# Loading expert weights in halves of 1 MB: one decoder layer on one Trainium2 core

## Chip, cores and metric

The kernel runs on one core of one Trainium2 chip. The metric is device time in microseconds (us) of one execution, the median over several. "The profiled execution" is one further execution, recorded by the hardware profiler; its span runs from the first to the last recorded instruction.

## What is computed

One layer of a decoder trunk: 256 tokens of 1024 float32 numbers, a conditioning vector `c`, a mixer (causal pooling beside a gated DeltaNet), then a mixture of experts, then a last RMSNorm. The change lies in the mixture of experts:

```python
def moe_ffn(h, router_w, router_b, w1, b1, w2, b2):
    logits = xt @ router_w + router_b                 # (256, 32)
    top_val, top_idx = lax.top_k(logits, 4)
    comb = softmax(top_val)
    ...                                               # tokens grouped by expert into blocks
    def expert_block(args):
        hu = xb @ w1[e] + b1[e]                       # w1[e]: 1024 x 2048
        x_glu = minimum(hu[:, 0::2], 7.0)
        x_lin = clip(hu[:, 1::2], -7.0, 7.0)
        act = x_glu * sigmoid(1.702 * x_glu) * (x_lin + 1.0)
        return act @ w2[e] + b2[e]                    # w2[e]: 1024 x 1024
    ...                                               # sum over experts, weighted by comb
```

All 32 experts have tokens, so all their weights are read: 12 MB (12.6 million bytes) for each expert, 403 MB in all, float32.

## The kernel before

**Staging.** Five engines run their own programs and meet at semaphores. All large weights pass through one SBUF buffer, `ring`: `RING` = 6 slots of 2 MB (128 partitions of 16 KB). SyncE issues the loads into it, in the order in which TensorE uses them. The front of the kernel (modulation, projections, mixer) takes 30 chunks through the ring, five uses of each slot (`USES` = 5). Then `stream(e, blocks_before)` loads one expert: slots 0 to 3 hold w1, two of its eight k-columns each (input features p*8+c, so one partition's two columns are 16 KB in a row in DRAM), slots 4 and 5 hold w2, half of its rows each, in two parts of 8 KB a partition.

**Semaphores.** `landed[s]` rises by 16 with each load into slot s, `used[s]` by 1 each time TensorE is done with it. SyncE waits for `used[s]` at the number of blocks before this expert plus `USES`, and issues the load (L503, L504). TensorE waits for `landed[s]` at 16 times the uses so far (L1343, L1365). The last expert's slots 3 and 5 are an exception: they are loaded in two halves of 1 MB (L501, L502), the second with a semaphore of its own, `hidden_in` and `last_in`.

**Order of the work.** The router's result is turned into a list of blocks of up to 64 tokens, in SBUF, on the chip (`blocks_i`); an expert with more than 64 tokens has a second block, which finds its weights in the ring. In this input there are 33 blocks for 32 experts (66 gates of two a block in the trace). TensorE runs `serve(n)` for each: the bias product, four `w1_chunk`s of eight products each (L1338; two records each in the trace, so "x16" is a chunk and "x64" a block's w1), `gather` of the next block's tokens (L1309), `combine` of the block before (L1384), the turns of selection, activation and next tokens (L1402, L1322, L1316), and two `w2_chunk`s of eight products (L1372). VectorE and ScalarE compute the gates between: the first gate when bank 0 is complete (`pe_hu`), the second when `used[3]` says that bank 1 is. `serve_last` is the last block, in a slightly other order. Expert 0's block stands before the loop, mixed with the last steps of routing.

**Small loads.** SyncE also loads the expert biases (`b_in`, four loads) and the last norm's weights (`fin_g`, semaphore `fin_in`); at the very start `c` (`c_in`) and the identity (`const_in`).

Of the kernel before, what the change touches and what calls it, by code (L numbers as in the profile page):

```python
# [24 lines left out]
P = 128  # L25
# [14 lines left out]
E = 32  # L40
# [3 lines left out]
RING = 6  # L44
# [13 lines left out]
ROW_C = 0  # L58
# [54 lines left out]
def program(nc, x, c, ada_w, ada_b, norm_mix_g, norm_ffn_g, w_in, conv_w, pool_w, pool_scale, a_log,  # L113
            dt_bias, gdn_norm_g, w_pool_out, w_gdn_out, w_out, router_w, router_b, exp_w1, exp_b1,
            exp_w2, exp_b2, final_norm_g, const, out):
    with ExitStack() as ctx:
# [148 lines left out]

        const_in = sem("const_in")
        rows_in = sem("rows_in")
        c_in = sem("c_in")
        tables_in = sem("tables_in")
        x_in = sem("x_in")  # L270
        early_in = sem("early_in")
        b_in = sem("b_in")
        fin_in = sem("fin_in")
        hidden_in = sem("hidden_in")
        last_in = sem("last_in")
        out_done = sem("out_done")
        landed = [sem(f"landed{i}") for i in range(RING)]
        upper_in = [sem(f"upper_in{i}") for i in range(2)]
        used = [sem(f"used{i}") for i in range(RING)]

        vec_chain = sem("vec_chain")
# [191 lines left out]

        @block.sync
        def _(sp):
            sp.dma_start(rows[ROW_C:ROW_C + 8, :], c.rearrange("b (r n) -> (b r) n", n=P)).then_inc(c_in, 16)
            sp.dma_start(consts[:, 0:2 * P + 1], const[:, 0:2 * P + 1]).then_inc(const_in, 16)
            for t in range(T):
                sp.dma_start(xt[:, t, :], x[0, t * P:(t + 1) * P, :]).then_inc(x_in, 16)
            for n, (kind, src) in enumerate(chunks):  # L480
                if n >= RING:
                    sp.wait_ge(used[n % RING], n // RING)
                dst = ring[:, n % RING, :, :]
                if kind in parts_of:
                    dst = slot_as(n % RING, parts_of[kind])
                if n in chunk_no["qkv"][:2]:
                    sp.dma_start(dst[:, 0:4, :], src[:, 0:4, :]).then_inc(upper_in[n - 2], 16)  # L487
                else:
                    sp.dma_start(dst, src).then_inc(landed[n % RING], 16)
                if n == RING - 1:  # L490
                    for m in chunk_no["qkv"][:2]:
                        sp.dma_start(ring[:, m, 4:8, :], chunks[m][1][:, 4:8, :]).then_inc(landed[m], 16)
                if n == RING - 1:
                    sp.dma_start(consts[:, 2 * P + 1:CONST_W], const[:, 2 * P + 1:CONST_W]).then_inc(tables_in, 16)

            def stream(e, blocks_before):
                for s in range(RING):
                    src = w1_dram[e, :, 2 * s:2 * s + 2, :] if s < 4 else w2_dram[e, s - 4]
                    sp.wait_ge(used[s], blocks_before + USES)
                    if isinstance(e, int) and e == E - 1 and s in (3, 5):  # L500
                        sp.dma_start(slot_as(s, 2)[:, 0, :], src[:, 0, :]).then_inc(landed[s], 16)  # L501
                        sp.dma_start(slot_as(s, 2)[:, 1, :], src[:, 1, :]).then_inc(hidden_in if s == 3 else last_in, 16)  # L502
                    else:  # L503
                        sp.dma_start(slot_as(s, 2), src).then_inc(landed[s], 16)  # L504

            stream(0, 0)
            sp.wait_ge(vec_x1, 4)
            for i in range(2):
                at = slice(i * SLOTS, i * SLOTS + E)
                sp.dma_start(b1_rows[at, :], exp_b1[0][:, i * D:(i + 1) * D]).then_inc(b_in, 16)  # L510
                sp.dma_start(b2_rows[at, :], exp_b2[0][:, i * 512:(i + 1) * 512]).then_inc(b_in, 16)
            sp.dma_start(fin_g, final_norm_g.partition_broadcast(P)).then_inc(fin_in, 16)
            sp.wait_ge(vec_route, 1)
            with sp.Fori(1, E - 1) as e:
                stream(e, first_block_of(sp, e))
            stream(E - 1, first_block_of(sp, E - 1))
            for i in range(2 * T):
                cut_ = slice((i % 2) * 512, (i % 2 + 1) * 512)
                sp.wait_ge(vec_out, i + 1)
                sp.dma_start(out[0, (i // 2) * P:(i // 2 + 1) * P, cut_], fin[:, i // 2, cut_]).then_inc(out_done, 16)  # L520
            sp.wait_ge(out_done, 16 * 2 * T)
# [267 lines left out]
        def _(pe):  # L789
# [41 lines left out]
                if i % 2:  # L831
                    mm.then_inc(pe_adacol, 1)

            pe.wait_ge(const_in, 16)
            pe.wait_ge(c_in, 16)
            nc.tensor.transpose(bank[7][:, 0:8], rows[ROW_C:ROW_C + 8, :], ident[0:8, 0:8]).then_inc(pe_c, 1)
            def keep_warm(times, b):

# [500 lines left out]
                                          slot_as(q, 2)[:, i, lo:lo + 512], start=False, stop=(c == KC - 1))  # L1339
                return mm  # L1340

            def w1_chunk(n, q, e=0, last=False):
                pe.wait_ge(landed[q], 16 * (e + USES + 1))  # L1343
                if q < 3:
                    for i in range(2):
                        for b in range(2):
                            mm = hidden(n, q, i, b)
                    mm.then_inc(used[q], 1)
                elif last:
                    for b in range(2):  # L1350
                        hidden(n, q, 0, b)
                    pe.wait_ge(hidden_in, 16)
                    hidden(n, q, 1, 0).then_inc(pe_hu, 1)
                    hidden(n, q, 1, 1).then_inc(used[q], 1)
                else:
                    for i in range(2):
                        mm = hidden(n, q, i, 0)
                    mm.then_inc(pe_hu, 1)
                    for i in range(2):
                        mm = hidden(n, q, i, 1)  # L1360
                    mm.then_inc(used[q], 1)

            def w2_chunk(n, b, e, last=False):
                pe.wait_ge(act_actT, 2 * n + b + 1)
                pe.wait_ge(landed[4 + b], 16 * (e + USES + 1))  # L1365
                for h in range(2):
                    if last and b and h:
                        pe.wait_ge(last_in, 16)
                    for c in range(2):
                        for o in range(2):  # L1370
                            lo = c * D + o * 512
                            mm = nc.tensor.matmul(bank[2][o * SLOTS:(o + 1) * SLOTS, :], actT[:, b, c, h, :],  # L1372
                                                  slot_as(4 + b, 2)[:, h, lo:lo + 512],
                                                  start=(b + h + c == 0), stop=(b + h + c == 3))
                mm.then_inc(used[4 + b], 1)

            def combine(n, last=False):

# [45 lines left out]
            def serve_last(n):  # L1424
                e = E - 1
                bias(n)
                w1_chunk(n, 0, e)
                w1_chunk(n, 1, e)
                combine(n - 1)
                w1_chunk(n, 2, e)  # L1430
                turn_sel(n)
                w1_chunk(n, 3, e, last=True)
                keep_warm(5, 3)
                turn_act(n, 0)
                keep_warm(2, 3)
                pe.wait_ge(act_selT, n + 1)
                w2_chunk(n, 0, e)
                turn_act(n, 1)
                w2_chunk(n, 1, e, last=True)

            keep_warm(2, 0)
            pe.wait_ge(pool_h2, 1)
# [3 lines left out]
                             start=True, stop=True).then_inc(pe_route, 1)  # L1446
            turn_x(0)
            keep_warm(2, 0)
            pe.wait_ge(b_in, 16 * 4)
            bias(0)  # L1450
            w1_chunk(0, 0)
            pe.wait_ge(vec_blocks, 2)
# [19 lines left out]
        def _(dve):  # L1472
# [375 lines left out]
            copy(blocks_i[:, 2 * P:2 * P + E], bank[6][0:1, 32:32 + E])  # L1848
            copy(blocks_i[:, 0:2 * P], bank[6][0:1, 64:64 + 2 * P]).then_inc(vec_route, 1)
            dve.wait_ge(act_gt2, 1)  # L1850
            dve.wait_ge(b_in, 16 * 4)
            for h in range(2):
                at = slice(h * SLOTS, h * SLOTS + E)
                ins = tt(b2_rows[at, :], b2_rows[at, :], gt2_row[at, :], ALU.mult)
# [18 lines left out]
            def serve(n, last=False):  # L1873
                e, start = (0, 0) if isinstance(n, int) else (expert_of(dve, n), start_of(dve, n))
                if not last:
                    e_next, start_next = expert_of(dve, n + 1), start_of(dve, n + 1)
                at_least(dve, pe_selT, n)
                for t in range(T):
                    ins = ts(wsel[:, t], slots[:, bass.ds(start, SLOTS)].unsqueeze(1).to_broadcast([P, 2, SLOTS]),  # L1879
                             slot_of[:, t, bass.ds(e, 1)], gatew[:, t, bass.ds(e, 1)], ALU.is_equal, ALU.mult)  # L1880
                ins.then_inc(vec_wsel, 1)
                dve.wait_ge(pe_gather, n + 1)
                if not last:
                    select(e_next, start_next)
                dve.wait_ge(pe_hu, n + 1)
                gated(n, 0)
                dve.wait_ge(used[3], n + USES + 1)
                gated(n, 1)
                if not last:
                    dve.wait_ge(pe_gather, n + 2)  # L1890
                    mark(e_next)
                dve.wait_ge(used[5], n + USES + 1)
                tt(y_nat, bank[2][:, :], gt2_row, ALU.mult).then_inc(vec_y, 1)  # L1893

            dve.wait_ge(vec_route, 1)
# [24 lines left out]
            add_experts(1, 0)  # L1920
            add_experts(1, 1)
            half_of_squares(1)
            dve.wait_ge(fin_in, 16)
            scale_out(0)
            scale_out(1)

# [26 lines left out]
```

## Time and profile before

| what | us |
|---|---|
| median of 3 runs | 1356.93 (1356.05 to 1356.97) |
| the profiled execution | 1355.68 |
| its span | 1353.3 |
| TensorE busy | 1282.3 (95% of the span) |
| VectorE, ScalarE, GpSimd busy | 391.3, 188.2, 48.3 |
| chain that ended last | TensorE 54%, DMA 42% |
| mean rate of all loads | 349 GB/s, 471.71 MB |

The page's rows by slice cut the span into 40 equal parts of 33.8 us. Busy shares add up over stages with different limits; the chain that ended last follows, from the last instruction back, what released each. A line such as L1338 is that of kernel.py. The granted TensorE clock is 0.997 of full speed over the span. "Landing" is the moment at which the last of the 16 DMA engines has raised the semaphore of a load.

### The profile page before, as it was taken

The page shows a single profiled execution, that of the slowest core. Times are in us where ns is not written, and L with a number is a line of the kernel's source. Part 1 is how long each engine was busy: PE and PEld are TensorE (multiplying, and loading weights), DVE is VectorE, ACT ScalarE, POOL GpSimd, SP SyncE. Part 2 cuts the span into 40 slices and gives each one's busy share as a digit, 9 for nine tenths or more (in the row PEclk, how much of TensorE's full clock was granted, in tenths as well). Part 3 has the DMA queues.
Part 4 walks back from the last instruction along what each step waited for, and adds up shares of the span by engine and source line. Part 5 has one row for each costly group of instructions (what it writes and reads, how often), then busy time and mean ns, then how long its engine had stood idle before and what let it go on. Part 6 is the DMA issues. An engine that isn't in the chain of part 4 may idle for free.

```text
span 1353.3 us, 17457 instructions
## 1 busy us (share of the span) xinstructions
PE 1282.3 (95%) x6549; PEld 624.1 (46%) x6550; DVE 391.3 (29%) x982; ACT 188.2 (14%) x401; POOL 48.3 (4%) x48
## 2 busy tenths in 40 slices
PE   7999999999999999989999998999999999999997
PEld 5788878898653333223333322333333322333332
DVE  1599574732252211112111111211211111121112
ACT  1110223422120110001100000100010000011001
POOL 1020012220000000000000000000000000000000
PEclk9999999999999999999999999999999999999999
DMA  9998550008349999999999999699999999999996
GB/s 334 357 375 299 206 187 1 1 27 316 124 152 407 426 426 426 425 426 426 428 426 426 426 425 426 253 427 423 426 429 426 426 427 425 426 425 429 427 426 248
DMA packets 69079, 471.71 MB, mean 349 GB/s; under 512 B 4093, under 2 KB 4410, under 8 KB 36154
## 3 DMA queue, kind: packets, MB, share of 16 engines
q1 hardware_dynamic: 68224, 469.62, 84.5%
q10 hardware_dynamic: 538, 1.13, 0.3%
q0 software_dynamic: 288, 0.55, 0.2%
q8 instruction: 21, 0.34, 0.1%
q14 instruction: 8, 0.07, 0.0%
HBM read 470.23 MB, written 1.05 MB: 348 GB/s over the span
## 4 chain that ended last, share of the span: by engine, by line
PE 54%; DMA 42%; DVE 1%; SPq 1%; ACT 1%; issue 1%; DVEq 0%
DMA ring<-in_exp_w_dram 40%; PE bank L1338 18%; PE bank L806 12%; PE bank L1372 6%; PE bank L1235 2%; DMA ring<-in_ada_w_dram 2%; PE bank L1024 2%; PE bank L1384 2%; PE bank L1309 2%; PE bank L900 1%; PE bank L1330 1%; PE bank L1157 1%; PE bank L1141 1%; PE bank L1154 1%; SPq L487 1%
## 5 line engine op out<-in xcount | busy, mean ns | idle before, releaser
L1338 PE MATMUL bank<-ring,work 128*64 128x512 f32 x2112 | 470.6, 596 | 47.3 <-DMA ring<-in_exp_w_dram 47.3
L1338 PEld LDWEIGHTS bank<-ring,work 128*64 128x64 f32 x2112 | 144.6, 137 | 368.9 <-issue 272.2
L1372 PE MATMUL bank<-ring,work 128*64 128x512 f32 x1056 | 234.1, 595 | 0.9 <-ACT work L749 0.5
L1372 PEld LDWEIGHTS bank<-ring,work 128*64 128x64 f32 x1056 | 72.9, 137 | 137.9 <-issue 136.6
L756 ACT ACTIVATE work<-work 128x256 f32<-128x256 f32 x66 | 27.5, 416 | 765.1 <-DVE work L1863 765.1
L1863 DVE TENSOR_SCALAR work<-bank 128x256 f32<-128x256 f32 x66 | 27.6, 419 | 350.4 <-PE bank L1338 350.4
L806 PE MATMUL bank<-region_h,ring 128*128 128x256 f32 x576 | 126.6, 380 | 0.0
L806 PEld LDWEIGHTS bank<-region_h,ring 128*128 128x128 f32 x576 | 108.8, 190 | 14.4
L1893 DVE TENSOR_TENSOR work<-bank,work 128x512 f32<-128x512 f32 x33 | 22.8, 692 | 313.8 <-PE bank L1372 313.8
L1384 PE MATMUL bank<-work 64*128 64x512 f32 x264 | 65.6, 615 | 0.8 <-DVE work L1893 0.8
L1309 PE MATMUL bank<-qkv,work 128*64 128x512 f32 x264 | 62.3, 592 | 0.2 <-DVE work L1801 0.2
L1879 DVE TENSOR_SCALAR work<-consts,region_z 128x128 f32 (+1 forms) x66 | 19.9, 345 | 87.7 <-issue 87.7
L1870 DVE TENSOR_TENSOR work<-work 128x256 f32<-128x256 f32 x66 | 40.7, 617 | 12.3 <-DVE work L1866 12.3
L1384 PEld LDWEIGHTS bank<-work 64*128 64x128 f32 x264 | 22.7, 186 | 43.2 <-issue 41.5
L1309 PEld LDWEIGHTS bank<-qkv,work 128*64 128x64 f32 x264 | 19.0, 137 | 37.4 <-issue 37.4
L1330 PE MATMUL bank<-work 32*64 32x512 f32 x264 | 35.9, 612 | 0.3 <-issue 0.3
L1505 DVE SCALAR_TENSOR_TENSOR region_z<-ring,c_act,region_z 128x512 f32<-128x512 f32 x48 | 35.6, 809 | 0.0
L1538 DVE SCALAR_TENSOR_TENSOR qkv<-bank,conv_cols,qkv 128x255 f32<-128x255 f32 (+2 forms) x72 | 31.3, 477 | 1.3
L900 PE MATMUL bank<-region_h,ring 128*128 128x256 f32 x128 | 28.8, 382 | 1.3 <-DVE region_h L1523 1.3
L1024 PE MATMUL bank<-region_h,ring 128*128 128x256 f32 x128 | 29.6, 379 | 0.0
L806 PE MATMUL bank<-region_z,ring 128*128 128x256 f32 x128 | 27.9, 380 | 1.0 <-DVE region_z L1736 1.0
L1866 DVE SCALAR_TENSOR_TENSOR work<-work 128x256 f32<-128x256 f32 x66 | 28.0, 425 | 2.3
(304 smaller groups left out, 953.6 us busy)
## 6 DMA issues: line engine op xcount, KB each, us to landing
ring<-in_exp_w_dram SPq DMA_DIRECT2D x190, 2048.0 KB, 23.6
ring<-in_ada_w_dram SPq DMA_DIRECT2D x12, 2048.0 KB, 12.4
ring<-in_w_in_dram SPq DMA_DIRECT2D x11, 2048.0 KB, 12.8
ring<-in_w_in_dram SPq DMA_DIRECT2D x4, 1024.0 KB, 17.2
ring<-in_w_gdn_out_dram SPq DMA_DIRECT2D x2, 2048.0 KB, 11.7
ring<-in_w_out_dram SPq DMA_DIRECT2D x2, 2048.0 KB, 16.6
ring<-in_exp_w_dram SPq DMA_DIRECT2D x4, 1024.0 KB, 23.5
ring<-in_w_pool_out_dram SPq DMA_DIRECT2D x1, 2048.0 KB, 8.4
```

The source lines that it names most:

```text
L806: mm = nc.tensor.matmul(out_ap, w(k) if w else w_slot(n, j, k), rhs[:, k, :], start=(k == 0), stop=(k == kc - 1))
L900: mm = nc.tensor.matmul(pair(i)[:, a, :], w_slot(n, 2 * (i % 2) + a, k), hT[:, k, :], start=(k + a == 0), stop=(k == KC - 1), skip_group_c ...
L1024: mm = nc.tensor.matmul(pair(7)[:, a, :], w_slot(n, j, k), hT[:, k, :], start=(k == 0), stop=(k == KC - 1))
L1309: mm = nc.tensor.matmul(bank[3][h * SLOTS:(h + 1) * SLOTS, :], sel[:, t, :], h2[:, t, h * 512:(h + 1) * 512], start=(t == 0), stop=(t == T ...
L1330: nc.tensor.matmul(bank[b][h * SLOTS:(h + 1) * SLOTS, :], onehot[b * SLOTS:b * SLOTS + E, :], b1_rows[b * SLOTS:b * SLOTS + E, h * 512:(h ...
L1338: mm = nc.tensor.matmul(bank[b][h * SLOTS:(h + 1) * SLOTS, :], xT[:, c % 4, c // 4, :], slot_as(q, 2)[:, i, lo:lo + 512], start=False, sto ...
L1372: mm = nc.tensor.matmul(bank[2][o * SLOTS:(o + 1) * SLOTS, :], actT[:, b, c, h, :], slot_as(4 + b, 2)[:, h, lo:lo + 512], start=(b + h + c ...
L1384: mm = nc.tensor.matmul(bank[4 + 2 * t + h][:, :], wselT[at, t * P:(t + 1) * P], y_nat[at, :], start=False, stop=last, skip_group_check=True)
L1505: ins = stt(half, w[:, k, :], c_act[:, k:k + 1], half, ALU.mult, ALU.add)
L1538: steps.append(stt(qkv[:, f, shift:S], src[:, a, 0:S - shift], w, qkv[:, f, shift:S], ALU.mult, ALU.add))
L1866: stt(lin[:, b, :], lin[:, b, :], 1.0, glu[:, b, :], ALU.add, ALU.mult).then_inc(vec_lin, 1)
L1870: tt(act_nat[:, b, :].rearrange("q (c p) -> q p c", c=2), lin[:, b, :].rearrange("q (p c) -> q p c", c=2), sig[:, b, :].rearrange("q (p c) ...
```

## The change

Each of the 32 experts' six slots is now loaded in two halves of 1 MB, and freed in two halves. A half of a w1 slot is one k-column, 128 rows of 8 KB that are 64 KB apart in DRAM; a half of a w2 slot is one of its two parts. The first half's load raises `landed[s]`, the second's a new semaphore `late_in[s]`, one for each slot. TensorE waits for each half by itself and raises `used[s]` after each, so twice for a block; the waits of SyncE and VectorE count accordingly. In slot 3 the products now go by k-column (both banks), not by bank, so that bank 0 is complete after six of eight products. The last expert is no longer a special case. `c_in` is joined with `const_in`, `fin_in` with `b_in`, and `hidden_in` and `last_in` are gone.

```diff
         def _(sp):
-            sp.dma_start(rows[ROW_C:ROW_C + 8, :], c.rearrange("b (r n) -> (b r) n", n=P)).then_inc(c_in, 16)
+            sp.dma_start(rows[ROW_C:ROW_C + 8, :], c.rearrange("b (r n) -> (b r) n", n=P)).then_inc(const_in, 16)
...
             def stream(e, blocks_before):
                 for s in range(RING):
                     src = w1_dram[e, :, 2 * s:2 * s + 2, :] if s < 4 else w2_dram[e, s - 4]
-                    sp.wait_ge(used[s], blocks_before + USES)
-                    if isinstance(e, int) and e == E - 1 and s in (3, 5):
-                        sp.dma_start(slot_as(s, 2)[:, 0, :], src[:, 0, :]).then_inc(landed[s], 16)
-                        sp.dma_start(slot_as(s, 2)[:, 1, :], src[:, 1, :]).then_inc(hidden_in if s == 3 else last_in, 16)
-                    else:
-                        sp.dma_start(slot_as(s, 2), src).then_inc(landed[s], 16)
+                    for i in range(2):
+                        sp.wait_ge(used[s], USES if isinstance(e, int) and e == 0 else 2 * blocks_before + (USES - 1 + i))
+                        sp.dma_start(slot_as(s, 2)[:, i, :], src[:, i, :]).then_inc(late_in[s] if i else landed[s], 16)
...
-            sp.dma_start(fin_g, final_norm_g.partition_broadcast(P)).then_inc(fin_in, 16)
+            sp.dma_start(fin_g, final_norm_g.partition_broadcast(P)).then_inc(b_in, 16)
...
-            def w1_chunk(n, q, e=0, last=False):
-                pe.wait_ge(landed[q], 16 * (e + USES + 1))
-                if q < 3:
-                    for i in range(2):
-                        for b in range(2):
-                            mm = hidden(n, q, i, b)
-                    mm.then_inc(used[q], 1)
-                elif last:
...
-                else:
-                    for i in range(2):
-                        mm = hidden(n, q, i, 0)
+            def half_arrived(s, e, i):
+                pe.wait_ge(late_in[s], 16 * (e + 1)) if i else pe.wait_ge(landed[s], 16 * (e + USES + 1))
+
+            def w1_chunk(n, q, e=0):
+                half_arrived(q, e, 0)
+                hidden(n, q, 0, 0)
+                hidden(n, q, 0, 1).then_inc(used[q], 1)
+                half_arrived(q, e, 1)
+                mm = hidden(n, q, 1, 0)
+                if q == 3:
                     mm.then_inc(pe_hu, 1)
-                    for i in range(2):
-                        mm = hidden(n, q, i, 1)
-                    mm.then_inc(used[q], 1)
-
-            def w2_chunk(n, b, e, last=False):
+                hidden(n, q, 1, 1).then_inc(used[q], 1)
+
+            def w2_chunk(n, b, e):
                 pe.wait_ge(act_actT, 2 * n + b + 1)
-                pe.wait_ge(landed[4 + b], 16 * (e + USES + 1))
                 for h in range(2):
-                    if last and b and h:
-                        pe.wait_ge(last_in, 16)
+                    half_arrived(4 + b, e, h)
...
-                mm.then_inc(used[4 + b], 1)
+                    mm.then_inc(used[4 + b], 1)
...
-            pe.wait_ge(b_in, 16 * 4)
+            pe.wait_ge(b_in, 16 * 5)
...
-                dve.wait_ge(used[3], n + USES + 1)
+                dve.wait_ge(used[3], 2 * n + (USES + 2))
```

SyncE's program in the loop over experts 1 to 30, slots 0, 1 and 4 (L504 before, L498 after; ISA rows compute the value that the wait compares with). Before:

```order
L504 ISA [waits used0]
L504 DMA ring<-in_exp_w1_dram 128x4096
L504 ISA [waits used1]
L504 DMA ring<-in_exp_w1_dram 128x4096
...
L504 ISA [waits used4]
L504 DMA ring<-in_exp_w2_dram 128x2x2048
```

And now:

```order
L498 ISA [waits used0]
L498 DMA ring<-in_exp_w1_dram 128x2048
L497 REGISTER_ALU
L498 ISA [waits used0]
L498 DMA ring<-in_exp_w1_dram 128x2048
L498 ISA [waits used1]
L498 DMA ring<-in_exp_w1_dram 128x2048
```

Each load of a slot has become two, each behind a wait of its own; the w1 loads go from 4096 numbers a partition (16 KB) to 2048.

TensorE's program in the loop over blocks, the last two w1 slots (L1338 before, L1331 after; bank0 and bank1 are the two halves of the hidden row). Before:

```order
L1338 MATMUL bank0<-ring,work 64x512 [waits landed2]
L1338 MATMUL bank0<-ring,work 64x512
L1338 MATMUL bank1<-ring,work 64x512 x2
L1338 MATMUL bank0<-ring,work 64x512 x2
L1338 MATMUL bank1<-ring,work 64x512 x2
L1338 MATMUL bank0<-ring,work 64x512 [waits landed3]
L1338 MATMUL bank0<-ring,work 64x512 x3
L1338 MATMUL bank1<-ring,work 64x512 x4
```

And now:

```order
L1331 MATMUL bank0<-ring,work 64x512 [waits late_in2]
L1331 MATMUL bank0<-ring,work 64x512
L1331 MATMUL bank1<-ring,work 64x512 x2
L1331 MATMUL bank0<-ring,work 64x512 [waits landed3]
L1331 MATMUL bank0<-ring,work 64x512
L1331 MATMUL bank1<-ring,work 64x512 x2
L1331 MATMUL bank0<-ring,work 64x512 [waits late_in3]
L1331 MATMUL bank0<-ring,work 64x512
L1331 MATMUL bank1<-ring,work 64x512 x2
```

Each group of four products has its own wait, and in slot 3 bank 0 gets its last product two later, sixth of eight in place of fourth.

## Rows read from the trace of the kernel before

**Rows 1.** page: busy time; GB/s by slice (span / 40)

```profile
PE 1282.3 (95%) x6549; PEld 624.1 (46%) x6550; DVE 391.3 (29%) x982; ACT 188.2 (14%) x401; POOL 48.3 (4%) x48
...
GB/s 334 357 375 299 206 187 1 1 27 316 124 152 407 426 426 426 425 426 426 428 426 426 426 425 426 253 427 423 426 429 426 426 427 425 426 425 429 427 426 248
```

**Rows 2.** chain in order of time, 570 to 612 us: start us, us, what

```profile
551.46 25.64 DMA ring<-in_exp_w_dram
...
580.97 25.65 DMA ring<-in_exp_w_dram
```

**Rows 3.** chain in order of time, around expert 15's second block

```profile
842.83 3.65 PE bank L1338 x16
...
851.36 7.02 PE bank L1372 x32
...
859.39 13.88 PE bank L1338 x64
...
886.19 13.88 PE bank L1338 x63
```

**Rows 4.** windows: us, busy us by engine, granted clock, DMA share, GB/s

```profile
429.50:842.80 413.30, 388.73 (x1862) 130.44 (x1858) 72.44 (x200) 41.38 (x98) 0.00 (x0) 1.00 1.01 426
852.60:864.80 12.20, 12.20 (x62) 3.84 (x60) 1.62 (x5) 0.00 (x0) 0.00 (x0) 1.00 0.08 20
870.40:1328.30 457.90, 435.16 (x2090) 146.85 (x2088) 81.39 (x222) 47.29 (x112) 0.00 (x0) 1.00 1.01 426
```

**Rows 5.** timeline of TensorE, 560 to 611 us: start us, us, line, [idle before <-releaser]

```profile
572.25 3.65 PE L1338 MATMUL bank<-ring,work 128*64 128x512 f32 x16 [1.03 <-DMA ring<-in_exp_w_dram]
577.15 3.65 PE L1338 MATMUL bank<-ring,work 128*64 128x512 f32 x16 [1.24 <-DMA ring<-in_exp_w_dram]
...
601.78 3.65 PE L1338 MATMUL bank<-ring,work 128*64 128x512 f32 x16 [1.04 <-DMA ring<-in_exp_w_dram]
```

**Rows 6.** the last expert's loads: slot 2 (L504), halves of 3 and 5 (L501, L502)

```profile
L504 SPq DMA_DIRECT2D ring<-in_exp_w_dram x1: 328/328/328, 1297.5 to 1297.5; - x1
...
DMA to landing us min/median/max: 25.8/25.8/25.8
...
L501 SPq DMA_DIRECT2D ring<-in_exp_w_dram x2: 328/328/328, 1302.4 to 1314.3; - x2
...
DMA to landing us min/median/max: 21.4/22.4/23.4
...
L502 SPq DMA_DIRECT2D ring<-in_exp_w_dram x2: 432/433/434, 1302.8 to 1314.7; - x2
...
DMA to landing us min/median/max: 23.5/24.5/25.5
```

**Rows 7.** SyncE's first load after the second block (L504, 863 to 864 us)

```profile
L504 SPq DMA_DIRECT2D ring<-in_exp_w_dram x1: 342/342/342, 863.2 to 863.2; - x1
...
DMA to landing us min/median/max: 7.3/7.3/7.3
```

**Rows 8.** timeline of TensorE, 1297 to 1345 us

```profile
1298.71 3.65 PE L1338 MATMUL bank<-ring,work 128*64 128x512 f32 x16 [1.24 <-DMA ring<-in_exp_w_dram]
...
1328.09 3.65 PE L1338 MATMUL bank<-ring,work 128*64 128x512 f32 x16
...
1338.98 3.65 PE L1372 MATMUL bank<-ring,work 128*64 128x512 f32 x16 [0.47 <-ACT work L749]
```

**Rows 9.** timeline of all engines in a block that waits for nothing

```profile
470.38 0.62 DVE L1870 TENSOR_TENSOR work<-work 128x256 f32<-128x256 f32 x1 [0.19 <-DVE work L1866]
...
473.18 0.38 PE L1322 MATMUL bank<-consts,work 128*128 128x128 f32 x2
```

**Rows 10.** fin_g's load (L512); TensorE's first bias products, 380 to 455 us

```profile
L512 SPq DMA_DIRECT2D work<-in_final_norm_g_dram x1: 423/423/423, 389.6 to 389.6; - x1
...
DMA to landing us min/median/max: 8.3/8.3/8.3
...
399.14 1.09 PE L1330 MATMUL bank<-work 32*64 32x512 f32 x8 [0.29 <-issue]
```

More of the change, by code:

```diff
@@ L267, in program @@
         rows_in = sem("rows_in")
-        c_in = sem("c_in")
         tables_in = sem("tables_in")
@@ L272, in program @@
         b_in = sem("b_in")
-        fin_in = sem("fin_in")
-        hidden_in = sem("hidden_in")
-        last_in = sem("last_in")
         out_done = sem("out_done")
@@ L278, in program @@
         upper_in = [sem(f"upper_in{i}") for i in range(2)]
+        late_in = [sem(f"late_in{i}") for i in range(RING)]
         used = [sem(f"used{i}") for i in range(RING)]
@@ L832, in ada_turned @@
                     mm.then_inc(pe_adacol, 1)
-            pe.wait_ge(const_in, 16)
-            pe.wait_ge(c_in, 16)
+            pe.wait_ge(const_in, 32)
             nc.tensor.transpose(bank[7][:, 0:8], rows[ROW_C:ROW_C + 8, :], ident[0:8, 0:8]).then_inc(pe_c, 1)
@@ L1340, in hidden @@
                 return mm
-            def w1_chunk(n, q, e=0, last=False):
-                pe.wait_ge(landed[q], 16 * (e + USES + 1))
-                if q < 3:
-                    for i in range(2):
-                        for b in range(2):
-                            mm = hidden(n, q, i, b)
-                    mm.then_inc(used[q], 1)
-                elif last:
[L1350 to L1354, printed above, removed]
-                else:
-                    for i in range(2):
-                        mm = hidden(n, q, i, 0)
+            def half_arrived(s, e, i):
[7 more added lines that the diff above has]
+                if q == 3:
                     mm.then_inc(pe_hu, 1)
-                    for i in range(2):
-                        mm = hidden(n, q, i, 1)
-                    mm.then_inc(used[q], 1)
-            def w2_chunk(n, b, e, last=False):
+                hidden(n, q, 1, 1).then_inc(used[q], 1)
+            def w2_chunk(n, b, e):
                 pe.wait_ge(act_actT, 2 * n + b + 1)
-                pe.wait_ge(landed[4 + b], 16 * (e + USES + 1))
                 for h in range(2):
-                    if last and b and h:
-                        pe.wait_ge(last_in, 16)
+                    half_arrived(4 + b, e, h)
                     for c in range(2):
@@ L1431, in serve_last @@
                 turn_sel(n)
-                w1_chunk(n, 3, e, last=True)
+                w1_chunk(n, 3, e)
                 keep_warm(5, 3)
@@ L1438, in serve_last @@
                 turn_act(n, 1)
-                w2_chunk(n, 1, e, last=True)
+                w2_chunk(n, 1, e)
             keep_warm(2, 0)
@@ L1850, in _ @@
             dve.wait_ge(act_gt2, 1)
-            dve.wait_ge(b_in, 16 * 4)
+            dve.wait_ge(b_in, 16 * 5)
             for h in range(2):
@@ L1891, in serve @@
                     mark(e_next)
-                dve.wait_ge(used[5], n + USES + 1)
+                dve.wait_ge(used[5], 2 * n + (USES + 2))
                 tt(y_nat, bank[2][:, :], gt2_row, ALU.mult).then_inc(vec_y, 1)
@@ L1922, in _ @@
             half_of_squares(1)
-            dve.wait_ge(fin_in, 16)
+            dve.wait_ge(b_in, 16 * 5)
             scale_out(0)
```

## Prediction, made before the changed kernel was run

> **What bounds the kernel now.** I read the page first: TensorE is busy for 95% of the span, yet the row of GB/s stands at 423 to 429 in nearly every slice from the thirteenth on, and it falls to 253 once past the middle [rows 1]. So both engines are nearly full, and the question is which of them sets the pace in which stretch.
>
> The chain in order of time answers it. In the middle of the stream its links are two DMAs of 25.64 and 25.65 us, 29.51 us apart from start to start (580.97 - 551.46) [rows 2]: one expert's 12.6 MB takes 29.5 us. TensorE needs 26.80 us for a block when it waits for nothing (859.39 to 886.19) [rows 3], 2.7 us less. From 429.5 to 842.8 us and from 870.4 to 1328.3 us the DMA engines are full at 426 GB/s; only in the 12.2 us from 852.6 is the queue nearly empty, 20 GB/s [rows 4]. There expert 15 has a second block of tokens: its last slot has landed, and no slot comes free until TensorE has reached that block's first chunk. Before and after it the queue is one unbroken row of transfers, and the time is its length, plus that hole, plus a tail.
>
> **Part 1, rows of 8 KB in place of 16 KB.** A w1 slot is now loaded as 128 rows of 16 KB (columns 2s and 2s+1 of a partition lie together in DRAM), a w2 slot as 256 rows of 8 KB. After the change all are halves of 128 rows of 8 KB. The trace has a price for this. TensorE waits for the slots 2 and 3 of an expert and starts each as it lands: 572.25 and 577.15, so a w1 slot takes 4.90 us. From slot 3 to the next expert's slot 2 it is 24.63 us, for two w2 and three w1 slots: (24.63 - 3 x 4.90) / 2 = 4.965 us for a w2 slot [rows 5]. The same bytes in 8 KB rows take 0.065 us more. The last expert's slot 3 is already loaded in two halves: slot 2 lands at 1297.5 + 25.8 = 1323.3, the halves at 1302.4 + 23.4 = 1325.8 and 1302.8 + 25.5 = 1328.3: 5.0 us for the slot, to a tenth [rows 6]. Bounds for the extra time are 0.05 and 0.10 us a slot (5.0 less 4.90 above); I take 0.075, nearer to the difference that is read to hundredths. It counts wherever the queue is full: 15 experts of 4 slots up to the second block, and 16 of 4 less the one that is halved already: 60 + 63 = 123 slots, **+9.2 us** (6.2 to 12.3). w2 slots keep their rows; their second semaphore I cost at nothing, since the halves of the last expert land 2.5 us apart like half a slot [rows 6].
>
> The Trainium skill, "DMA: Bandwidth & Descriptors", section "Why small descriptors are slow (HBM only)", puts the fixed cost of a packet at about 3 cycles beside one per 32 bytes, and calls packing of use only at 256 bytes and below. By it two rows of 8 KB cost 518 beats for 515, an estimate of 0.03 us a slot, 3.5 us in all, and the sum would come out 1.5 us below no change. The trace does not agree: it shows more than twice that between the two kinds of slot.
>
> **Part 2, the hole at the second block.** TensorE starts slot 3 of expert 15 at 842.83, as it lands, and reaches the second block's first chunk 16.56 us later (859.39) [rows 3]; SyncE issues the next load at 863.2, when all eight products of slot 0 are done, and it lands 7.3 us after [rows 7]. Four chunks take 13.88 us, so one takes 3.47 and half of one 1.73. After the change the first half of slot 3 is worked off before the second lands, so everything up to the second block stands 1.73 us nearer to the landing; and slot 0's first half is given back after half a chunk, 1.73 us sooner. Nothing on the way turns late: the w2 slots land 5.0 and 9.9 us after slot 3; TensorE starts on them 8.53 us after taking slot 3 up (851.36), so then 6.8 us after the landing, and wants their second halves 8.5 and 12.0 us after it [rows 3, 5]. **-3.5 us**; it cannot be more, since nothing is freed earlier, and the least is one of the two alone, -1.7. Elsewhere early freeing brings nothing: loads wait 22 to 26 us in the queue already (the 25.64 of [rows 2]), of which 4.9 is their own.
>
> **Part 3, the tail.** TensorE last waits for a load at 1298.71, slot 3 of expert 30, then works through without a gap to slot 3 of the last expert at 1328.09, whose second half it takes at 1329.8; that half had landed at 1328.3 [rows 6, 8]. So TensorE is 1.5 us late there, having begun at 1298.71 on a whole slot. With halves it begins 1.73 us nearer to the landing. Its own way from second half to second half is 1329.8 - 1300.4 = 29.4 us, DMA's is then 29.8, so it waits some 0.4 us for that half and the tail runs from the landing: **-1.5 us** (0 to -1.5). The second half of slot 5 then lands 9.9 us after it and is wanted 10.9 us after it (1338.98 + 1.73 - 1329.8) [rows 6, 8].
>
> **What is covered.** In slot 3 bank 0 is now complete after 6 of 8 products in place of 4, so VectorE starts 0.9 us later against TensorE's end. In a block that waits for nothing it ends both gates at 471.0, and TensorE turns the second at 473.18 [rows 9]: 2.2 us of cover; were it gone, a block of 26.8 us would take 27.7, still under the 29.5 of the queue. The six more waits of a block on TensorE and the loads that SyncE issues (12 for 6, 0.34 us each [rows 7], some 5 us in 29.5) hide behind running work. fin_g now counts in b_in: it lands at 389.6 + 8.3 = 397.9, TensorE's bias product starts at 399.14 [rows 10]; twelve issues for six put it back by some 0.4 us at most, within 1.2. The joined semaphore at the very start holds two loads that both were waited for.
>
> **Sum.** +9.2 - 3.5 - 1.5 = +4.2 us, from +1.2 to +7.3 by the bounds on the row's price. Against the profiled execution (1355.68, span 1353.3) that is 1359.9. The median of the runs is 1.25 us higher, 1356.93, so I forecast **1361.1**, 0.3% slower. A measurement can tell about 0.2%, 2.7 us.
>
> **Rivals.**
> - *The row length is free* (the other side). w2 slots may be slower for where their bytes lie, not for their rows. Then parts 2 and 3 alone remain: -5.0 us, 1351.9, faster. For it: w1 halves keep w1's layout. Against it: the last expert's halved w1 slot took 5.0 us like the w2 slots [rows 6]. It decides when the extra time is under 0.02 us a slot, where 123 slots cost less than 2.5 us.
> - *Half of it is the row length*: 0.035 us a slot, +4.3 - 5.0 = -0.7, 1356.2, no change. It needs both readings of part 1 to be too high. The Trainium skill's rule quoted in part 1 would end in the same case.
> - *Each further DMA costs too*, besides its rows: 0.02 us for each of 190 more (384 less 194), the room that 5.0 leaves over 4.965. Then +3.8 more, 1364.9.
> - *The hole closes by half only*, if a wait of VectorE or SyncE takes the place of the freed one: 1362.8 (1361.1 + 1.7).
> - *A completion stops the queue.* A load into an idle queue takes 7.3 us where one in the row takes 4.9 [rows 5, 7]; if each of the 190 paid these 2.4 us, 456 us in all, it would be 1817. The last expert's halves, 2.5 us apart, speak against it. The Trainium skill, on the same page, section "Anatomy of one DMA — SWDGE (gpsimd) path", gives a fixed 2.0 us for each DMA, by its figures 380 us; the trace shows it as a delay of the first, not of the row.
>
> **How the numbers follow.** Forecast 0.70, of which 0.64 lies above +2.7 us and 0.06 within (a price of 0.06 or less). Free rows 0.07, half 0.10, dearer DMAs 0.09, half a hole 0.03, stopped queue 0.01. Faster 0.07; same 0.06 + 0.10 = 0.16; slower 0.64 + 0.09 + 0.03 + 0.01 = 0.77. The range runs from the second rival, 1356.2 and a little below it (1356.0), to the third, 1365.0; the forecast's own is 1358.1 to 1364.2. Left out are the free rows, the stopped queue and the outermost bounds.
>
> **What would show it.** In the chain of the changed kernel the period of an expert reads 29.8 us in place of 29.51, and GB/s 422 in place of 426. TensorE waits for second halves, in all about 3.0 us a block. The load after the second block is issued 16.9 us after expert 15's last w1 half is taken up, not 20.4. The span ends 25.0 - 1.5 = 23.5 us after the last w1 half lands. A period of 29.5 would make the first rival right and the forecast wrong; a hole that stays at 12 us, or any new wait of TensorE on ScalarE or VectorE in a block, would break part 2.

## The result, and the profile after

| | before | after |
|---|---|---|
| median of 6 runs each, us | 1356.51 (1355.51 to 1357.76) | 1361.89 (1361.10 to 1365.63) |
| ratio, 95% interval | | 1.0042 (1.0031 to 1.0053) |
| the profiled execution, us | 1355.68 | 1361.10 |
| its span | 1353.3 | 1358.9 |

The change costs 5.4 us, 0.42%. The forecast was 1361.1, +4.2 us.

The page of the changed kernel, busy time and GB/s by slice, against [rows 1]:

```profile
PE 1291.7 (95%) x6549; PEld 619.5 (46%) x6550; DVE 390.8 (29%) x982; ACT 184.8 (14%) x401; POOL 48.3 (4%) x48
...
GB/s 333 358 376 302 199 183 1 1 44 298 124 155 422 421 422 422 422 421 422 421 422 423 421 421 423 281 423 421 422 422 422 422 422 422 422 422 422 422 422 262
```

The stream runs at 422 GB/s where it ran at 426, and the slice with the hole moved more, 281 for 253. Its chain in order of time, 500 to 860 us (start us, us, what):

```profile
571.91 1.96 SPq L498
...
574.18 3.29 SPq L498
...
701.41 26.54 DMA ring<-in_exp_w_dram
...
761.05 26.54 DMA ring<-in_exp_w_dram
...
820.68 26.54 DMA ring<-in_exp_w_dram
```

The chain now meets a load of the same place only at every second expert, so the steps are two experts: 59.64 and 59.63 us, 29.82 us each, where [rows 2] have 29.51. In between it runs over TensorE and over SyncE's own issues (SPq L498), 2 to 3 us each. SyncE's loads from 560 to 620 us (durations in ns, min/median/max), before (L504) and after (L498):

```profile
L504 SPq DMA_DIRECT2D ring<-in_exp_w_dram x13: 332/342/384, 559.9 to 619.0; - x13
...
DMA to landing us min/median/max: 22.1/24.0/25.7
```

```profile
L498 SPq DMA_DIRECT2D ring<-in_exp_w_dram x24: 333/1898/3286, 561.2 to 619.2; - x24
...
DMA to landing us min/median/max: 23.4/26.0/27.5
```

To issue a load of 1 MB takes SyncE 1.9 us in the median where the loads land 26 us later, for 0.34 before. The part on the prediction comes back to this.

TensorE's timeline in the stream, the halves of slots 2 and 3 of an expert, against [rows 5]:

```profile
571.32 1.94 PE L1331 MATMUL bank<-ring,work 128*64 128x512 f32 x8 [0.51 <-DMA ring<-in_exp_w_dram]
573.80 1.94 PE L1331 MATMUL bank<-ring,work 128*64 128x512 f32 x8 [0.55 <-DMA ring<-in_exp_w_dram]
```

It waits for each of these four halves. They start 2.49 us apart and take 1.73 of work each, so some 3.0 us are waited in a block, the sign that the prediction named (the rows show 0.5 of each 0.76, since a record of eight products runs on to the modelled end of its last). The windows (us; busy us of PE, PEld, DVE, ACT, POOL; granted clock; DMA share; GB/s) answer to [rows 4]:

```profile
429.50:847.30 417.80, 394.85 (x1872) 128.63 (x1868) 72.37 (x200) 39.85 (x98) 0.00 (x0) 1.00 1.01 422
857.10:865.00 7.90, 7.90 (x42) 2.38 (x40) 1.12 (x3) 0.00 (x0) 0.00 (x0) 1.00 0.00 0
857.10:865.90 8.80, 8.80 (x46) 2.67 (x44) 1.62 (x5) 0.00 (x0) 0.00 (x0) 1.00 0.08 15
872.70:1335.30 462.60, 441.50 (x2098) 145.11 (x2094) 81.30 (x222) 45.53 (x112) 0.00 (x0) 1.00 1.01 422
1335.30:1358.90 23.60, 13.80 (x66) 5.58 (x66) 9.87 (x21) 6.40 (x17) 0.00 (x0) 0.89 0.47 191
```

The queue is as full as before, at a lower rate. The nearly empty stretch is 8.8 us at 15 GB/s, where [rows 4] have 12.2 at 20: 3.4 us shorter. Now what lies around this hole. The chain around expert 15's second block, against [rows 3]:

```profile
847.27 1.94 PE bank L1331 x8
...
854.08 7.02 PE bank L1355 x32
...
862.11 13.88 PE bank L1331 x64
```

TensorE takes up the last half of slot 3 at 847.27 and is at the second block's first chunk 14.84 us later, for 16.56. SyncE's first two loads after it (L498, in the windows 864 to 865 and 865.5 to 866.5 us), against [rows 7]:

```profile
L498 SPq DMA_DIRECT2D ring<-in_exp_w_dram x1: 336/336/336, 864.2 to 864.2; - x1
...
DMA to landing us min/median/max: 4.8/4.8/4.8
...
L498 SPq DMA_DIRECT2D ring<-in_exp_w_dram x1: 333/333/333, 865.9 to 865.9; - x1
...
DMA to landing us min/median/max: 6.8/6.8/6.8
```

The first half is issued 16.9 us after the 847.27, as forecast (20.4 before). It lands at 869.0. The second lands at 872.7, 3.7 us after it, where the stream's pace is 2.5: this was not forecast. The rate between these two landings, and 2 us later:

```profile
869.00:872.70 3.70, 3.70 (x20) 1.26 (x18) 0.00 (x0) 0.00 (x0) 0.00 (x0) 1.00 0.95 352
...
875.00:880.00 5.00, 5.00 (x26) 1.82 (x23) 3.48 (x9) 1.32 (x3) 0.00 (x0) 1.00 1.01 426
```

The DMA engines were busy for 95% of the time there, but moved 352 GB/s, not the 422 of the stream. And the end, TensorE's timeline, against [rows 8]:

```profile
1333.20 1.94 PE L1331 MATMUL bank<-ring,work 128*64 128x512 f32 x8
1335.35 1.94 PE L1331 MATMUL bank<-ring,work 128*64 128x512 f32 x8 [0.22 <-DMA ring<-in_exp_w_dram]
...
1344.52 1.94 PE L1355 MATMUL bank<-ring,work 128*64 128x512 f32 x8 [0.47 <-ACT work L743]
```

TensorE waits 0.22 us for the last half of w1, then the tail runs from its landing. Side by side, from the rows of both traces:

| stretch | before | after | difference | forecast |
|---|---|---|---|---|
| to expert 15's last w1 (842.8; 847.3) | 842.8 | 847.3 | +4.5 | +4.5 (60 slots) |
| from there to slot 0 landed whole | 27.7 | 25.4 | -2.3 | -3.5 |
| from there to the last w1 half landed | 457.8 | 462.6 | +4.8 | +4.7 (63 slots) |
| from there to the end | 25.0 | 23.6 | -1.4 | -1.5 |
| span | 1353.3 | 1358.9 | +5.6 | +4.2 |

The texts of the experiments reckon with 0.077 us a slot, as the two traces give it: (29.82 - 29.51) / 4.

### The profile page after: what moved, and what is told of

It is laid out like the page before. It is cut to its first block, busy times and chain, and to the rows that moved or that the text cites. A ratio compares the mean times of both kernels' runs of the same rounds, so it can differ in the third digit from the quotient of the medians.

```text
span 1358.9 us, 18068 instructions
## 1 busy us (share of the span) xinstructions
PE 1291.7 (95%) x6549; PEld 619.5 (46%) x6550; DVE 390.8 (29%) x982; ACT 184.8 (14%) x401; POOL 48.3 (4%) x48
## 3 DMA queue, kind: packets, MB, share of 16 engines
q10 hardware_dynamic: 538, 1.13, 0.2%
## 4 chain that ended last, share of the span: by engine, by line
PE 60%; DMA 25%; SPq 11%; DVE 1%; issue 1%; ACT 1%; DVEq 0%
DMA ring<-in_exp_w_dram 24%; PE bank L1331 16%; PE bank L800 12%; PE bank L1355 11%; SPq L498 10%; PE bank L1367 3%; PE bank L1302 3%; PE bank L1228 2%; DMA ring<-in_ada_w_dram 2%; PE bank L1017 2%; PE bank L1323 2%; PE bank L893 1%; PE bank L1150 1%; PE bank L1134 1%; PE bank L1147 1%
## 5 line engine op out<-in xcount | busy, mean ns | idle before, releaser
L1331 PE MATMUL bank<-ring,work 128*64 128x512 f32 x2112 | 479.7, 598 | 44.1 <-DMA ring<-in_exp_w_dram 44.1
L1331 PEld LDWEIGHTS bank<-ring,work 128*64 128x64 f32 x2112 | 139.9, 136 | 379.3 <-issue 248.4
L1355 PE MATMUL bank<-ring,work 128*64 128x512 f32 x1056 | 234.1, 595 | 0.9 <-ACT work L743 0.5
L1846 DVE TENSOR_SCALAR work<-bank 128x256 f32<-128x256 f32 x66 | 27.5, 417 | 383.6 <-PE bank L1331 383.6
L750 ACT ACTIVATE work<-work 128x256 f32<-128x256 f32 x66 | 27.5, 417 | 798.2 <-DVE work L1846 798.2
L1355 PEld LDWEIGHTS bank<-ring,work 128*64 128x64 f32 x1056 | 72.9, 137 | 137.9 <-issue 136.3
## 6 DMA issues: line engine op xcount, KB each, us to landing
ring<-in_w_out_dram SPq DMA_DIRECT2D x2, 2048.0 KB, 16.9
```

Source lines behind the costliest of these rows:

```text
L1331: mm = nc.tensor.matmul(bank[b][h * SLOTS:(h + 1) * SLOTS, :], xT[:, c % 4, c // 4, :], slot_as(q, 2)[:, i, lo:lo + 512], start=False, sto ...
```

## Experiments

Each ran on one chip beside the kernel before, whose median over its runs there is given. The changed kernel itself ran beside none of them, so its 1361.89 is compared over the two medians of the kernel before (1356.51 there, 1356.57 to 1357.16 here). Two theories stood: the row length is what costs, and halves give something back at two places; against it, that the number of loads or of semaphores costs, or that halves give nothing. Profiles differ by up to 3.1 us in the time at which the first expert load after routing is issued (405.8 to 408.9 us), with no order by the edits; spans are compared from there.

### Rows of 8 KB alone

```diff
-                    src = w1_dram[e, :, 2 * s:2 * s + 2, :] if s < 4 else w2_dram[e, s - 4]
+                    src = w1_dram[e, :, s:s + 5:4, :] if s < 4 else w2_dram[e, s - 4]
...
-                c = 2 * q + i
+                c = q + 4 * i
```

> The kernel before, with one edit: a w1 slot holds the columns s and s+4 of each partition in place of 2s and 2s+1, so one load of 2 MB is 256 rows of 8 KB; nothing is loaded or freed in halves. If the row length is what costs (theory): a w1 slot takes 4.97 us in place of 4.90, an expert 29.8 us in place of 29.5, and the time is 120 x 0.077 = 9.2 us longer, about 1365.7. If the number of loads or of semaphores costs (rival): 29.5 us and 1356.5, no change.

Measured: 1366.30 beside 1356.76, ratio 1.0071 (1.0058 to 1.0084). Its chain in order of time, 570 to 640 us:

```profile
555.04 25.96 DMA ring<-in_exp_w_dram
584.87 25.94 DMA ring<-in_exp_w_dram
614.69 25.93 DMA ring<-in_exp_w_dram
```

An expert takes 29.83 and 29.82 us, with the same number of loads, of semaphores and of waits as before the change. From the first load after routing (408.0) to the end (1364.8) it is 956.8 us, before the change 947.2 (406.1 to 1353.3): +9.6, for 9.2 expected. The medians say the same, 9.5 us. The row length alone makes the whole price. The rows of this run lie 32 KB apart in DRAM, those of the changed kernel 64 KB, and they take 29.82 us an expert in both.

### Halves loaded, whole slots waited for and freed

```diff
                 half_arrived(q, e, 0)
-                hidden(n, q, 0, 0)
-                hidden(n, q, 0, 1).then_inc(used[q], 1)
                 half_arrived(q, e, 1)
+                hidden(n, q, 0, 0)
+                hidden(n, q, 0, 1)
...
-                    for i in range(2):
-                        sp.wait_ge(used[s], USES if isinstance(e, int) and e == 0 else 2 * blocks_before + (USES - 1 + i))
+                    sp.wait_ge(used[s], blocks_before + USES)
+                    for i in range(2):
...
```

> The changed kernel's loads in halves, but TensorE waits for both halves of a slot and frees the whole slot, as before the change. Theory: the price of the rows alone, 9.2 us, and 0.4 for the last expert's slot 3 taken up whole: about 1366.1, and the idle stretch of the queue after expert 15 is back at its length before (18 us from the last landing to the next slot's). The difference to the changed kernel, about 4 us, is what waiting and freeing in halves gives. Rival (arrival in halves gives nothing, the queue hides it): as the changed kernel, 1361.9.

Measured: 1364.72 beside 1356.76, ratio 1.0064 (1.0051 to 1.0076). In its chain an expert takes 29.82 us (585.01 - 555.19):

```profile
555.19 25.35 DMA ring<-in_exp_w_dram
585.01 25.37 DMA ring<-in_exp_w_dram
```

From its first load (407.7) to its end (1364.5) it is 956.8 us, the same as with 8 KB rows in whole loads (the medians of four runs each are 1364.72 and 1366.30): 190 further loads and their semaphores add nothing that can be measured. Against the changed kernel's 953.0 (405.9 to 1358.9) waiting and freeing in halves is worth 3.8 us in the traces, 2.8 between the medians; this run's profiled execution was the longest of its four (1366.85), so 2.8 is the better figure. The rival that the queue hides all of it falls.

### w1 whole in rows of 16 KB, w2 in halves

```diff
+                    if s < 4:
+                        sp.wait_ge(used[s], blocks_before + USES)
...
+                            sp.dma_start(slot_as(s, 2), src).then_inc(landed[s], 16)
+                        continue
                     for i in range(2):
...
```

> The changed kernel with its w1 slots loaded whole in rows of 16 KB and freed whole, w2 slots in halves. Theory: an expert takes 29.5 us again, no gain at the second block and none in the tail, 1356.5, as before the change. Rival (each further load costs 0.02 us): 64 more loads, 1357.8.

Measured: 1356.53 beside 1356.76, ratio 0.9997 (0.9984 to 1.0009). The chain's step is back at 29.52 us (582.13 - 552.61):

```profile
552.61 25.65 DMA ring<-in_exp_w_dram
582.13 25.68 DMA ring<-in_exp_w_dram
```

Halving a slot whose rows are 8 KB anyway costs nothing that can be measured, and brings nothing either.

### Two loads for a w1 slot, rows of 16 KB

```diff
...
+                    elif s < 4:
+                        for i in range(2):
+                            at = slice(i * HALF, (i + 1) * HALF)
+                            sp.dma_start(slot_as(s, 2)[at], src[at]).then_inc(late_in[s] if i else landed[s], 16)
...
```

> The kernel before, with each w1 slot loaded by two loads of 64 partitions, rows of 16 KB, each with its own semaphore; TensorE waits for both and frees whole slots. Theory (row length): an expert takes 29.5 us, about 1356.7 (0.2 for the last expert's slot 3, which is no longer waited for by column). Rival (each load costs, 0.077 us a slot for one more load): 29.8 us, about 1366.

Measured: 2030.68 (2003.94 to 2154.89) beside 1356.76. Both theories missed by far. The window from 1300 to 1900 us:

```profile
1300.00:1900.00 600.00, 417.55 (x1566) 137.36 (x1568) 62.69 (x168) 35.48 (x84) 0.00 (x0) 0.82 1.01 253
```

The DMA engines are as busy as ever and move 253 GB/s in place of 426. A pair of loads into 64 partitions each does not do here what one load into 128 does. So this run says nothing on the number of loads; the two before it do.

### Only slot 3 in halves

```diff
+                    if s < 3:
+                        sp.wait_ge(used[s], blocks_before + USES)
+                        sp.dma_start(slot_as(s, 2), src).then_inc(landed[s], 16)
+                        continue
...
```

> The changed kernel with only slot 3 and the two w2 slots in halves; slots 0 to 2 whole, rows of 16 KB. Theory: rows cost 30 x 0.077 = +2.3 us; expert 15's slot 3 still arrives in halves, -1.7; the tail still gains 1.5: -0.9 in all, 1355.6. If the tail gain came from slots 0 to 2 too (rival), it is lost: 1357.1.

Measured: 1356.82 beside 1357.16, ratio 0.9999 (0.9990 to 1.0008). The interval holds both the theory's -0.9 us and the rival's +0.6, so the times don't decide between them; the trace does. TensorE's timeline in the last block, and the loads of the last expert's slot 3 (L502):

```profile
1316.27 3.65 PE L1335 MATMUL bank<-ring,work 128*64 128x512 f32 x16
1321.05 3.65 PE L1335 MATMUL bank<-ring,work 128*64 128x512 f32 x16 [1.13 <-DMA ring<-in_exp_w_dram]
...
1326.55 3.65 PE L1335 MATMUL bank<-ring,work 128*64 128x512 f32 x16
...
1330.50 3.65 PE L1335 MATMUL bank<-ring,work 128*64 128x512 f32 x16
```

```profile
L502 SPq DMA_DIRECT2D ring<-in_exp_w_dram x2: 327/328/328, 1301.7 to 1303.5; - x2
...
DMA to landing us min/median/max: 26.6/27.0/27.4
```

It now waits 1.13 us for slot 1, which comes whole, and is at slot 3's second half at 1332.2 (1330.50 + 1.73), again after it has landed (1303.5 + 27.4 = 1330.9). In the trace the rival holds: the tail's gain needs slots 0 to 2 in halves as well, because a TensorE that is nearer to the landings meets a whole slot too early.

### Slot 0's halves issued together; slot 0 alone in halves

```diff
-                        sp.wait_ge(used[s], USES if isinstance(e, int) and e == 0 else 2 * blocks_before + (USES - 1 + i))
+                        if s or not i:
+                            first = USES - 1 + i if s else USES
+                            sp.wait_ge(used[s], USES if isinstance(e, int) and e == 0 else 2 * blocks_before + first)
```

> The changed kernel, with SyncE waiting until all of slot 0 is free before it issues its two halves, one right after the other. In the changed kernel the second half of slot 0 landed 3.70 us after the first behind the second block, where 2.49 is the pace. If that is because the second load was issued 1.7 us after the first, into a short queue (theory): now both land 2.0 to 2.5 us apart, 0.3 us later than in the changed kernel, about 1362.2. If not (rival), the later issue costs its full 1.7 us: 1363.6.

Measured: 1362.06 beside 1357.16, ratio 1.0037 (1.0024 to 1.0050); the changed kernel had 1.0042. Its two loads behind the hole (L500):

```profile
L500 SPq DMA_DIRECT2D ring<-in_exp_w_dram x2: 333/335/337, 865.7 to 866.2; - x2
...
DMA to landing us min/median/max: 4.8/5.7/6.7
```

Issued 0.5 us apart, they land at 870.5 and 872.9, 2.4 us apart. Counted from where TensorE takes up slot 3's last half (847.05 here, 847.27 in the changed kernel), the first lands 1.7 us later than in the changed kernel, the second 0.4. So freeing slot 0 in halves wins 0.4 us there, of 1.73. Between these two landings the stream ran at its full pace:

```profile
870.50:872.90 2.40, 2.40 (x14) 0.82 (x12) 0.00 (x0) 0.00 (x0) 0.00 (x0) 1.00 1.00 423
```

The other way round, with slots 1 to 3 whole:

```diff
+                    if 0 < s < 4:
+                        sp.wait_ge(used[s], blocks_before + USES)
...
+                            sp.dma_start(slot_as(s, 2), src).then_inc(landed[s], 16)
+                        continue
...
```

> The changed kernel with slot 0 and the w2 slots in halves, slots 1 to 3 whole in rows of 16 KB and freed whole. Rows cost 30 x 0.077 = +2.3 us. Behind the second block slot 0's first half is issued 1.7 us before its second. Theory (what was seen in the changed kernel holds for any load issued that long after the first into an idle queue): the second half lands 3.7 us after the first, not 2.5, so only 0.5 us is won there: 1358.5. Rival (it was chance): 2.5 us after it, 1.7 us won, 1357.3.

Measured: 1358.67 beside 1356.57, ratio 1.0016 (1.0007 to 1.0025). Its two loads (L506):

```profile
L506 SPq DMA_DIRECT2D ring<-in_exp_w_dram x2: 333/334/336, 862.9 to 864.6; - x2
...
DMA to landing us min/median/max: 4.8/5.9/7.0
```

Issued 1.7 us apart they land at 867.7 and 871.6, 3.9 apart, at 401 GB/s in between. The late second half is there in both traces with this spacing, so it was hardly chance. Why it is late was not found.

### The last block's combine after slot 3

```diff
                 w1_chunk(n, 1, e)
-                combine(n - 1)
                 w1_chunk(n, 2, e)
-                turn_sel(n)
                 w1_chunk(n, 3, e, last=True)
-                keep_warm(5, 3)
+                combine(n - 1)
+                turn_sel(n)
                 turn_act(n, 0)
```

> The kernel before, where the last block's combine of the block before it (1.9 us of products) and the turn of the selection stand after slot 3, in place of five idle products. Theory: TensorE, which was 1.5 us late at the last expert's slot 3, is now there as its second half lands; the combine fits into the wait for the gates but for 0.4 us: -1.1 us, 1355.4. Rival (the tail is set by the gates and the last slot's landing): no change, 1356.5, or up to 0.4 us slower.

Measured: 1355.73 beside 1357.16, ratio 0.9994 (0.9983 to 1.0005), not clear of zero. In the trace, from taking up slot 3 of expert 30 (1298.44) to the end (1352.1) it is 53.7 us; before the change it was 54.6 (1298.71 to 1353.3). TensorE's timeline:

```profile
1323.07 7.09 PE L1338 MATMUL bank<-ring,work 128*64 128x512 f32 x32 [1.04 <-DMA ring<-in_exp_w_dram]
1330.09 1.99 PE L1384 MATMUL bank<-work 64*128 64x512 f32 x8
```

It now waits for a load within the last block, so the tail begins at a landing, with slots 0 to 2 whole. In this trace it is two thirds of part 3's gain without the change; the medians can't confirm it.

### The joined semaphores alone

```diff
...
-            pe.wait_ge(const_in, 16)
-            pe.wait_ge(c_in, 16)
+            pe.wait_ge(const_in, 32)
...
-            pe.wait_ge(b_in, 16 * 4)
+            pe.wait_ge(b_in, 16 * 5)
...
```

> The kernel before with its c and fin_g loads counted in their neighbours' semaphores, nothing else. Theory: no change, 1356.5; TensorE's first bias product still starts at 399 us. Rival (fin_g's landing holds it up): up to 1 us slower.

Measured: 1355.91 beside 1357.16, ratio 0.9993 (0.9984 to 1.0002). TensorE's first bias product:

```profile
398.81 1.09 PE L1327 MATMUL bank<-work 32*64 32x512 f32 x8 [0.29 <-issue]
```

It waits for no DMA there. The joins cost nothing that can be measured.

### w2 in rows of 16 KB

If 8 KB rows are what costs, the kernel before still pays for them in its w2 slots.

```diff
-        w2_dram = exp_w2.rearrange("l e (b h p c) n -> (l e) b p h (c n)", b=2, h=2, p=P)
+        w2_dram = exp_w2.rearrange("l e (b p h c) n -> (l e) b p h (c n)", b=2, h=2, p=P)
...
+            def fours(a, h):
+                return a.rearrange("p (m h j) -> p m h j", h=2, j=4)[:, :, h, :]
...
-                                          slot_as(q, 2)[:, i, lo:lo + 512], start=False, stop=(c == KC - 1))
+                                          fours(slot_as(q, 2)[:, i, b * D:(b + 1) * D], h), start=False, stop=(c == KC - 1))
```

> The kernel before, with its w2 slots in rows of 16 KB: partition p of a slot takes four rows of w2 that lie together (b*512 + 4p to 4p + 3) in place of two and two, and the products of w1 and of its biases read their columns in fours (every second group of four) so that the hidden features come out in the order that this needs. All whole loads are then 128 rows of 16 KB. Theory (0.077 us for each slot in 8 KB rows): an expert takes 29.37 us in place of 29.52, 56 w2 slots on the path save 0.073 us each, -4.1 us, 1352.6. Rival 1 (a w2 slot is slower for another reason than its rows): 29.52 us, no change, 1356.7. Rival 2 (reading columns in fours slows TensorE, so that a block exceeds 29.4 us): slower than 1356.7.

Measured: 1353.24 beside 1356.57, ratio 0.9975 (0.9965 to 0.9985). Its chain, 570 to 640 us, and a block of TensorE's that waits for nothing:

```profile
551.93 25.50 DMA ring<-in_exp_w_dram
581.30 25.49 DMA ring<-in_exp_w_dram
```

```profile
455.88 13.95 PE L1340 MATMUL bank<-ring,work 128*64 128x512 f32 x64
...
482.68 13.95 PE L1340 MATMUL bank<-ring,work 128*64 128x512 f32 x64
```

29.37 us an expert, as expected to the hundredth, and a block is still 26.80: reading the columns in fours costs TensorE nothing. A w2 slot's 2 MB lie in one piece in DRAM in both kernels, so where the bytes of a slot lie has not changed, only how they are cut into rows. With the late combine:

> w2_rows16 and late_combine together. Theory: -4.1 and -0.9 us, 1351.7. Rival (the two overlap in the tail): as w2_rows16.

Measured: 1352.48 beside 1356.57, ratio 0.9964 (0.9952 to 0.9976). It is 4.1 us faster than the kernel before, and by the medians 9.4 us faster than the changed kernel. Its lead over w2_rows16, 0.8 us, is within the intervals.

## Why the prediction was right

- **Part 1 held.** 0.075 us a slot was taken; the step of 29.82 in place of 29.51 gives 0.077, and the two stretches of the stream show +9.3 for +9.2. The row length was isolated by the first experiment, and the reverse, longer rows for w2, took 0.07 us off each w2 slot. The rival that row length is free, and the one that takes half of it, are refuted. The Trainium skill's 3 cycles a packet ("DMA: Bandwidth & Descriptors", "Why small descriptors are slow (HBM only)"), by which 0.03 us a slot was estimated, fall short of the trace's 0.077 by more than half. The same section also counts 32 bytes of descriptor, which the prediction left out; with them the estimate is 0.04, about half of the measured.
- **Dearer loads** were not: 190 more of them cost nothing measurable, by the second and third experiment.
- **Part 2 was mis-sized**: -3.5 forecast, -2.3 measured. The term that failed is the second 1.73 us, slot 0 given back in halves. The issue came when forecast, 16.9 us after, and the hole itself shrank by 3.4; what was assumed is that the second half lands 2.5 us behind the first. It landed 3.7 behind, while the queue moved 352 GB/s. The first 1.73, TensorE nearer to the landing, held. This is nearly all that the forecast of +4.2 lacks to the 5.4 and 5.6 measured; the rival "the hole closes by half only" (1362.8) is about as near to the measured 1361.89 as the forecast of 1361.1 is, but no wait of VectorE or SyncE took the place of the freed one. Why the second half is late stays open.
- **Part 3 held**: -1.4 for -1.5, with a wait of 0.22 us where 0.4 was reckoned. What the text did not say is that it hangs on slots 0 to 2 arriving in halves too, as the trace with slot 3 alone in halves shows.
- **What is covered** stayed covered: the trace shows no new wait of TensorE on VectorE or ScalarE in a block, and alone the joined semaphores cost nothing that can be measured. But one term of it was mis-sized: SyncE's 12 loads were reckoned at 0.34 us each, some 5 us in 29.5. That holds behind the hole (0.33); in the full stream SyncE issues for 18.7 us of one expert's 29.8 (the 12 loads from 587.6 to 611.7). The issues of loads that land 23.4 and 24.2 us later take 0.33 us, those of loads that land 25.0 to 27.5 us later 0.5 to 3.1. It cost nothing: with whole waits the same loads take 0.33 us in the median (560 to 680 us), and an expert takes 29.82 us as well. That it stayed covered is no merit of the 5 us that were reckoned. Why an issue takes longer was not tried.
- **The range**, 1356.0 to 1365.0, also holds the rivals of half the price (1356.2) and of dearer loads (1364.9). The time alone would not have told them from the forecast; the rows and experiments did.

## What to carry to other kernels

Where a transfer queue sets the pace, look at how long the rows are before splitting a load: here a split that halves the rows, 16 KB to 8, was paid at every load, and the shorter wait was won only where the queue had run dry and at the end. Two kinds of load that move the same bytes at a different pace in one trace are a price list; here it also named the better edit, the one that made the slower kind like the faster. Part of what a finer wait gains at the end may be had by moving other work behind the wait; one trace here shows it, the medians don't.

## What the runs showed of the hardware

- 128 rows of 16 KB and 256 rows of 8 KB, both 2 MB into 128 partitions: 4.90 and 4.97 us in a full queue (29.37 and 29.82 us for six); 120 such loads make 9 us.
- Loads of 1 MB into 64 partitions brought the stream to 253 GB/s from 426, with the DMA engines busy all the time. The Trainium skill, "DMA: Bandwidth & Descriptors", section "The descriptor swizzle", says that partitions 0 to 63 and 64 to 127 are written through different ports of SBUF, eight each; a load of 64 partitions would then have half of them, which agrees in size: with 8 of an expert's 12 MB at half of 426 GB/s the mean would be 256, an estimate, for 253 measured. No run here tried another choice of 64.
- Two loads of 1 MB into an idle queue: issued 0.5 us apart they landed 2.4 us apart, issued 1.7 us apart 3.7 and 3.9. In the queue 9 to 12 us deep, issues 1.7 us apart gave 2.5.
- SyncE's issue of a load of 1 MB in rows of 8 KB took 0.33 us where the load landed within 21 us, and 1.9 in the median, up to 3.3, in a stretch where it landed 23.4 to 27.5 us later. In the kernel before, loads of 2 MB took 0.34 us in the median, 0.38 at most, with 22 to 26 us to the landing.
